# Output projections and late fillers of a two-block transformer kernel: from one fp32 product to three products of split operands, with GpSimd making the fillers' low parts

## The reference

```python
h = rms_norm(x); parts = split(h @ w_in)              # layer 0: a_u a_v a_g, b_q b_k b_v b_g, m_q m_g
x = x + concat([y_a, y_b, y_m], -1) @ w_out           # layer 0 (out0), w_out is 1280 x 1024
h = rms_norm(x); parts = split(h @ w_in)              # layer 1: c_a c_b c_g, d_q d_kv d_g, m_q m_g
x = x + concat([y_c, y_d, y_m], -1) @ w_out           # layer 1 (out1)
x = x + mix(retention(x), rg_lru(x)) @ w_out_2        # block 2
x = x + (gelu(conv(h @ up_g)) * (h @ up_v)) @ down    # feed-forward, then a last rms_norm
```

## Time and profile before

| | |
|---|---|
| median of 3 runs | 931.94 us (930.04 to 932.48) |
| the profiled execution | 932.02 us, of which 930.2 us lie between its first and last instruction |
| TensorE busy with matmuls | 889.6 us, 96% of the span |
| VectorE, ScalarE, GpSimd busy | 587.6, 389.7, 103.2 us |
| granted TensorE clock, mean | 0.992 |

### The profile page before, as it was taken

How to read it: one execution, slowest core, us unless ns; L and a number is a source line. 1 busy time by engine, 2 the same in 40 slices (tenths; PEclk the granted TensorE clock), 3 DMA queues, 4 the chain that set the end, 5 groups by cost and what they waited for, 6 DMA issues and landing times.

```text
span 930.2 us, 15618 instructions
## 1 busy us (share of the span) xinstructions
PE 889.6 (96%) x6262; PEld 824.1 (89%) x6262; DVE 587.6 (63%) x1114; ACT 389.7 (42%) x703; POOL 103.2 (11%) x114
## 2 busy tenths in 40 slices
PE   6999999999999999999999999999999999999996
PEld 6998988788888777878899999999998999999994
DVE  4784686432788788721597458955665676676673
ACT  6456654012002155612445676445354344543451
POOL 0149660101011000200400000100000000000000
PEclk9999999999999899999999999999999999999999
DMA  9444323243433611140655243555453456645641
GB/s 368 162 176 137 94 89 113 114 159 116 176 138 137 268 50 46 47 151 1 227 172 191 91 136 137 181 185 177 159 188 115 147 169 220 206 157 183 223 140 46
DMA packets 37784, 139.38 MB, mean 150 GB/s; under 512 B 4304, under 2 KB 4432, under 8 KB 37456
## 3 DMA queue, kind: packets, MB, share of 16 engines
q1 hardware_dynamic: 37424, 136.90, 42.5%
q10 hardware_dynamic: 288, 1.48, 0.5%
HBM read 137.32 MB, written 1.05 MB: 149 GB/s over the span
## 4 chain that ended last, share of the span: by engine, by line
PE 79%; issue 8%; DVE 8%; ACT 3%; POOL 1%; DMA 1%; DVEq 0%; SPq 0%; ACTq 0%; POOLq 0%
PE psum L534 18%; PE psum L535 18%; PE psum L536 18%; PE psum L537 18%; PE psum L609 1%; PE psum L667 1%; PE psum L685 1%; ACT logits L1195 1%; PE psum L810 1%; DVE neg_max L1803 1%; DVE psum L1797 1%; PE psum L678 1%; POOL w_lo L2253 1%; DVE rows L1834 1%; DMA rows<-in_mem 1%
## 5 line engine op out<-in xcount | busy, mean ns | idle before, releaser
L1546 DVE TENSOR_TENSOR w_lo<-raw,w_hi 128x1024 fp32r<-128x1024 f32 x162 | 190.9, 1222 | 76.4 <-ACT w_hi L1107 75.5
L534 PE MATMUL psum<-first 128*128 128x256 f32 (+1 forms) x960 | 218.6, 385 | 4.9 <-ACT first L1145 2.2
L534 PEld LDWEIGHTS psum<-first 128*128 128x128 f32 x960 | 180.5, 194 | 31.2 <-ACT first L1145 2.8
L1107 ACT ACTIVATE w_hi<-raw 128x1024 fp32r<-128x1024 f32 x184 | 185.8, 1053 | 34.5 <-PE psum L537 26.2
L535 PE MATMUL psum<-h_hi,w_hi 128*128 128x256 f32 x704 | 199.5, 283 | 0.6 <-issue 0.6
L537 PE MATMUL psum<-h_hi,w_lo 128*128 128x256 f32 x704 | 199.2, 283 | 0.0
L536 PE MATMUL psum<-h_lo,w_hi 128*128 128x256 f32 x704 | 199.2, 283 | 0.0
L535 PEld LDWEIGHTS psum<-h_hi,w_hi 128*128 128x128 f32 x704 | 135.1, 192 | 1.6 <-issue 1.4
L536 PEld LDWEIGHTS psum<-h_lo,w_hi 128*128 128x128 f32 x704 | 135.1, 192 | 0.2
L537 PEld LDWEIGHTS psum<-h_hi,w_lo 128*128 128x128 f32 x704 | 135.1, 192 | 0.0
L535 PE MATMUL psum<-w_hi,h_hi 128*128 128x256 f32 x448 | 129.5, 289 | 0.0
(11 more groups left out here) (268 smaller groups left out, 1071.5 us busy)
## 6 DMA issues: line engine op xcount, KB each, us to landing
raw<-in_blocks SPq DMA_DIRECT2D x184, 512.0 KB, 4.2
first<-in_blocks SPq DMA_DIRECT2D x64, 512.0 KB, 4.5
w_late<-in_blocks SPq DMA_DIRECT2D x4, 512.0 KB, 5.7
early<-in_early SPq DMA_DIRECT2D x1, 1579.0 KB, 16.4
attention<-in_late ACTq DMA_DIRECT2D x1, 1376.0 KB, 6.7
rows<-in_mem SPq DMA_DIRECT2D x2, 512.0 KB, 4.3
x<-in_x SPq DMA_DIRECT2D x1, 1024.0 KB, 8.4
out_x<-h_rows SPq DMA_DIRECT2D x2, 512.0 KB, 2.6
```

Source lines behind the costliest of these rows:

```text
L534: return nc.tensor.matmul(out, lhs[0], rhs[0], start=start, stop=stop, skip_group_check=shared_bank)
L1107: nc.scalar.activation(split_part(w_hi, q), raw[:, q % RAW_SLOTS, :], ACT.Copy).then_inc(w_hi_ready, 1)
L1546: V.tensor_tensor(split_part(w_lo, q), raw[:, q % RAW_SLOTS, :], split_part(w_hi, q).bitcast(F32), ALU.subtract).then_inc(w_lo_vector, 1)
```

## The change

The ten halves of `out0` and `out1` and the four of `c_g` and `d_g` move from `WHOLE` to `HALVES`: they become split products. Their left operands are split too. `ya`, `yb` and `ym` are copied to a high part by ScalarE (`source_hi`), all of them, and VectorE makes the low part behind it (`source_lo`, two instructions for a pair of tiles). For the fillers, layer 1's `h` stays whole for the other projections (now in the block of `mem_t`); ScalarE copies it to `h_hi`, and GpSimd makes `h_lo` in eight operations behind the power of the norm `dk`. `kv1` stays a whole product but is loaded through `raw` (`RAW_WHOLE`). GpSimd makes the low parts of `c_g`, `d_g`, `out0_r`, `out0` 0, `out1_r`, `out1` 0 and no longer of the first three halves of `x_lru`, which VectorE takes over with the other `out` halves; `out0` 1 stands inside the norm `y_b`. Layer 1's fillers begin two units later (`FILL_FROM`).

```diff
+FILL_FROM = [0, 2]
-LOW_BESIDE_NORM = {"q": both_of(["m_qg0"]), "k": both_of(["b_v"])}
+LOW_BESIDE_NORM = {"q": both_of(["m_qg0"]), "k": both_of(["b_v"]), "y_b": [("out0", 1)]}
...
-WHOLE = (both_of(["kv0"]) + out_halves(0)
-         + both_of(["kv1"]) + CONV_IN + both_of(["d_q", "dkv1", "m_qg1", "cmp_w1", "dkv2", "c_g", "d_g"]) + out_halves(1))
-HALVES = (L0_SPLIT + both_of(["x_lru0", "x_lru1", "r_q", "r_k", "y_lru0", "y_lru1", "r_v0", "r_v1", "g_ret0", "g_ret1"]
+WHOLE = both_of(["kv0"]) + CONV_IN + both_of(["d_q", "dkv1", "m_qg1", "cmp_w1", "dkv2"])
+RAW_WHOLE = both_of(["kv1"])
+HALVES = (L0_SPLIT + out_halves(0) + RAW_WHOLE + both_of(["c_g", "d_g"]) + out_halves(1) + both_of(["x_lru0", "x_lru1", "r_q", "r_k", "y_lru0", "y_lru1", "r_v0", "r_v1", "g_ret0", "g_ret1"]
...
-WHOLE_RING = [9, 4, 5, 6, 7]
+WHOLE_RING = [4, 5, 6, 7, 2, 3]
...
-VECTOR_FROM = len(L0_SPLIT) + SPLIT_SLOTS
-VECTOR_LO = both_of(["b_q", "b_k", "m_qg0", "b_v"]) + HALVES[VECTOR_FROM:]
+GPSIMD_LO = both_of(L0_FILL + ["c_g", "d_g"]) + [("out0_r", 0), ("out0", 0), ("out1_r", 0), ("out1", 0)]
+LO_BY_NAME = both_of(["b_q", "b_k", "m_qg0", "b_v"]) + [("out0", 1)]
...
-    return min(total, total * (i + 1) // FILL_UNITS[layer])
+    return min(total, total * max(0, i + 1 - FILL_FROM[layer]) // (FILL_UNITS[layer] - FILL_FROM[layer]))
```

TensorE, `out_rest` (`out_project` likewise goes from `y_whole` to `h_t`), and the new wait ahead of layer 1's attention:

```diff
-                                          pick(h_whole, slice(None), k, slice(t * P, (t + 1) * P)),
+                                          pick(ym_t, slice(None), k, slice(t * P, (t + 1) * P)),
...
+            pe.wait_ge(h1_lo, 1)
```

ScalarE at layer 0's end:

```diff
-            source("ym0", h_whole[0][:, 0:2, :], 0.5)
-            source("ya0_0", y_whole[0][:, 0:2, :], 0.25)
-            source("yb0_0", y_whole[0][:, 4:6, :], 0.5 * (1.0 - LAM_INIT))
+            split_to(OUT[0] + 3)
+            source_hi("ym0", ym_t[0], 0.5)
+            for j in range(2):
+                source_hi(f"ya0_{j}", h_t[0][:, 2 * j:2 * j + 2, :], 0.25)
+            split_to(OUT[0] + 4)
+            for j in range(2):
+                source_hi(f"yb0_{j}", h_t[0][:, 4 + 2 * j:6 + 2 * j, :], 0.5 * (1.0 - LAM_INIT))
+            split_to(OUT[0] + 5)
```

ScalarE in layer 1's projections:

```diff
+            for n in range(2):
+                k = slice(n * KT // 2, (n + 1) * KT // 2)
+                ins = nc.scalar.activation(h_t[0][:, k, :], h_whole[0][:, k, :], ACT.Copy)
+            src_hi.mark(ins, "h1", act)
...
+            split_to(FILL1 + 1)
             for j, name in enumerate("kv"):
                 arrive(xpose, f"hid_{name}")
...
+            split_to(FILL1 + 2)
             copy_chunk("dkv2", rows[:, :, 1024:1304], (HC, 24))
+            split_to(FILL1 + 3)
             nc.scalar.activation(gates[:, :, :], rows[:, :, 1280:1304], ACT.Tanh, scale=0.5).then_inc(gates_tanh, 1)
```

VectorE at layer 0's end (layer 1's likewise):

```diff
-            source("ya0_1", y_whole[0][:, 2:4, :], 0.25)
+            source_lo("ym0", ym_t, 0, 0.5)
+            for j in range(2):
+                source_lo(f"ya0_{j}", h_t, 2 * j, 0.25)
...
-            source("yb0_1", y_whole[0][:, 6:8, :], 0.5 * (1.0 - LAM_INIT))
+            split_to(OUT[0] + 4)
+            for j in range(2):
+                source_lo(f"yb0_{j}", h_t, 4 + 2 * j, 0.5 * (1.0 - LAM_INIT))
+            split_to(OUT[0] + 5)
             recurrence_rate()
```

GpSimd, behind each power:

```diff
+                if name == "dk":
+                    src_hi.wait(pool, "h1")
+                    for k in range(KT):
+                        ins = nc.gpsimd.tensor_tensor(h_t[1][:, k, :], h_whole[0][:, k, :], h_t[0][:, k, :].bitcast(F32),
+                                                      ALU.subtract)
+                    ins.then_inc(h1_lo, 1)
```

More of the change, by code:

```diff
@@ L102, with split_turn, split_before, hi_count @@
 MEM_BLOCK = 8
-WHOLE_RING = [9, 4, 5, 6, 7]
+WHOLE_RING = [4, 5, 6, 7, 2, 3]
 WHOLE_BLOCK = [9, 5] + [WHOLE_RING[j % len(WHOLE_RING)] for j in range(len(WHOLE) - 2)]
 WHOLE_TURN = [WHOLE_BLOCK[:j].count(b) for j, b in enumerate(WHOLE_BLOCK)]
-def split_slot(j):
-    return (j + 2) % SPLIT_SLOTS
+OUT = [HALVES.index(out_halves(layer)[0]) for layer in range(2)]
+X2 = HALVES.index(("x_lru0", 0))
+FILL1 = HALVES.index(("c_g", 0))
+SPLIT_HALVES = [h for h in HALVES if h not in RAW_WHOLE]
+def split_turn(j):
+    return SPLIT_HALVES.index(HALVES[j])
+def split_slot(j):
+    return (split_turn(j) + 2) % SPLIT_SLOTS
+def split_before(j):
+    n = split_turn(j) - SPLIT_SLOTS
+    return HALVES.index(SPLIT_HALVES[n]) if n >= 0 else None
+def hi_count(q):
+    return 2 * split_turn(q // 2) + q % 2 + 1
 def whole_ahead(j):
@@ L433, in low_parts, with raw_left @@
         def low_parts(q):
-            mine = HALVES[q // 2] in VECTOR_LO
-            ahead = sum((h in VECTOR_LO) == mine for h in HALVES[:q // 2])
-            return (w_lo_vector if mine else w_lo_ready), 2 * ahead + q % 2 + 1
+            pool = HALVES[q // 2] in GPSIMD_LO
+            ahead = sum((h in GPSIMD_LO) == pool for h in SPLIT_HALVES[:split_turn(q // 2)])
+            return (w_lo_ready if pool else w_lo_vector), 2 * ahead + q % 2 + 1
+        def raw_left(q):
+            return half_done[q // 2] if HALVES[q // 2] in RAW_WHOLE else low_parts(q)
         def wait_half(eng, half):
@@ L1047, in load_whole @@
                 if 2 <= block < MEM_BLOCK and 2 <= j and (ahead is None or ahead < 2):
-                    last = max(i for i in range(len(L0_SPLIT)) if split_slot(i) == (block - 2) // 2)
+                    last = max(i for i in range(FILL1) if HALVES[i] not in RAW_WHOLE and split_slot(i) == (block - 2) // 2)
                     sp.wait_ge(*half_done[last])
@@ L1481, in split_to @@
                 while split[0] < min(n, len(HALVES)):
-                    j = split[0]
+                    half = HALVES[split[0]]
                     split[0] += 1
-                    if j >= VECTOR_FROM:
-                        own_low_parts(HALVES[j])
+                    if half in SPLIT_HALVES and half not in GPSIMD_LO and half not in LO_BY_NAME:
+                        own_low_parts(half)
             def arrive(ring, name):
```

93 lines of the change are left out of this document (54 added, 39 removed).

## The result

The changed kernel takes **951.6 us** against 931.0 (ratio 1.020, interval 1.018 to 1.022): slower, as forecast, but by 19 to 20 us and not by 7, and outside the range. The 951.6 is the median of four executions, one of which took 3958 us at a mean granted clock of 0.21; the ratio leaves it out, and the other three took 947.6 to 952.7 us, 950.5 in the middle. So what follows explains the 15.3 us by which the two profiled spans differ. The mean granted clock was 0.969 to 0.973 in the three executions of the first series and is 0.975 in the profiled one; more time at the lower clock may be the missing 3 us, but no trace shows it.

The account below looks back on a forecast made before the run. TensorE, busy for 96% of the span, was taken as the bound, except ahead of layer 1's attention, where VectorE's program sets the time. The terms summed to +6.7 on 932.0 us, so 938.7, range 927 to 945.

Parts of the forecast that it names:

- Products, -16.1: TensorE: fourteen halves turned from whole to split products, 1.15 us less each, 16.1 us less work.
- Handovers, +3.7: Layers' ends: high and low parts replace single copies, lengthening three TensorE waits by about 1.2 us each, +3.7.
- Late weights, +1.4: Layer 0: `out0_2`'s low parts come 1.1 us late; two more ScalarE high parts in its attention cost 0.3.
- Start of the attention, +12: Ahead of layer 1's attention: four GpSimd bursts delay VectorE, 0.48 us per instruction hit, +12 us in all.
- the fourth burst: GpSimd's eight operations for `d_g` 0 ahead of layer 1's attention, perhaps half of them hitting VectorE, +2 us.
- The sign of 6 to 9 us idle ahead of the first scores: Check in the trace: TensorE would stand 6 to 9 us ahead of layer 1's first attention scores.
- Inside layer 1's attention, +3: First units without fillers, about 2 us; three pairs of ScalarE high parts, about 0.3 each; GpSimd bursts; +3 (1 to 6).
- Norm x2, -0.7: Layer 1's end: GpSimd's low parts no longer run beside VectorE's diagonal in the norm x2, -0.7 us.
- The clock, +3.4: TensorE's clock drops behind two of three lengthened handovers, 1.7 us each, +3.4 (0 to 6.8).
- the low parts did not slip in: Rival that GpSimd's low parts slip in beside VectorE, a hit costing a quarter: 927 us, chance 0.18.
- the whole-instruction price: Rival that a GpSimd instruction blocks VectorE for its whole length, 0.69 us a hit, start 18: 944.7 us, chance 0.12.

Follow-up runs that it names:

- h_lo_early: parts_behind_copy with `h_lo` made 60 us earlier, right after x1 is turned, so its GpSimd burst leaves the start of layer 1's attention; 935.4 us.
- late_behind: parts_behind_copy with the fillers' high parts made later on ScalarE, so GpSimd's bursts for `c_g` 0, `c_g` 1 and `d_g` 0 begin after `kc_t`; 943.7 us.
- one_pair_back: parts_behind_copy with one of its five pairs put back: `out1_r`'s high parts again ahead of the copy for unit 34 in layer 1's attention; 944.3 us.
- parts_behind_copy: Changed kernel with five pairs of ScalarE high parts in the two attentions moved behind one copy each of the transposed scores; 937.6 us.
- clock_kept: Changed kernel with plain matmuls, results unused, put on TensorE in six of its waits; 952.4 us.
- outs_only: Changed kernel with only output projections split: fillers whole, no `h_lo`, block order changed, high parts of `out1_r` and `out1` 0 later; 936.0 us.
- start_kept: parts_behind_copy with plain matmuls, written to a free bank, in four TensorE waits at the start of layer 1's attention; 942.4 us.
- vector_parts: parts_behind_copy with the low parts of `c_g` and `d_g` made by VectorE instead of GpSimd; 948.2 us.
- before_delayed: Kernel before the change, with two idle ScalarE copies ahead of one copy in each layer's attention (units 14 and 34), no product changed; 941.3 us.

## Why the prediction was off

- **Products, -16.1:** right. 144 records took 17.51 us at full clock (17.3 forecast).
- **Handovers, +3.7:** right. The waits are 1.99 us at both layers (2.1 forecast), and 1.70 instead of 0.79 ahead of `out1_r` (+0.9; 1.2 forecast).
- **Late weights, +1.4: the first step that failed,** in its second half. "Two more high parts fall on ScalarE in layer 0's attention ... +0.3" was an average over six pieces of before. What counts is between which instructions a piece stands: this one stood ahead of a copy that TensorE was about to need, behind a wait of 1.60 us that the trace of before showed. It cost 1.86 us, and 1.5 of clock. The average was also misapplied: 1.5 us over six pieces is 0.5 for two, not 0.3. `out0_2` cost 2.0 instead of 1.1.
- **Start of the attention, +12:** right in size and in what bounds it, 11.7. Inside it two errors met: the fourth burst cost 0.7 and not 2, and the slow clock lengthened VectorE's chain by 0.8, for which there was no term. The sign of 6 to 9 us idle ahead of the first scores did not hold (2.31). h_lo_early shows the price of one burst alone (3.4 us), late_behind that of the other three together with the clock (9.0).
- **Inside layer 1's attention, +3: the second and larger failure.** "About 0.3 each" for three pairs of high parts. They cost 0.48 us, 1.48 us and nothing as waits; what the term left out is that the clock comes down around such a wait. The second of them, with the low stretch around it, made 5.5 us (one_pair_back against parts_behind_copy), and with the clock held up the attention was 5.4 us shorter (clock_kept). With all five pairs behind their copies D to E is 83.3 us, where my terms give 82.2.
- **Norm x2, -0.7:** E to F is within 0.4 of the forecast; the diagonal takes 0.48 us, as in the earlier trace rows without GpSimd.
- **The clock, +3.4:** one drop behind a handover does cost about what I took (E to F is 38.2 us in outs_only, where it falls there, and 36.7 in the change; 1.5 against 1.7). But I put the drops in the wrong places, and took each to be 1.7 us wherever it falls. In the profile of the change none fell at a lengthened handover, and one stretch inside layer 1's attention lasted 17 us.

The two failures are one, a piece of work priced by an average and not by its place: 3.1 + 7.6 us. Changing the order takes 3.4 and 6.4 of them back, and the kernel then measures 937.6 us, where my sum was 938.7. The nearness is partly luck: the late weights and the attention come out about 1 us dearer each than summed, and the clock's 3.4 were not lost where I put them. Of the rivals, the low parts did not slip in, and hits of about 0.5 us fit better than the whole-instruction price: a rope instruction went from 0.22 to 0.76 us, and with 18 us the start would have been 115 us long, not 109.

Left open: why the clock fell late at layer 0's end in some executions and not in others with the same program there, and why the low stretch around the wait of 2.08 us lasts 3.4 us in some traces and 13.6 to 17 in others.

## What to carry to other kernels

Before you add work to an engine that is "40% busy", look between which two of its instructions it will stand, and who waits for the second one; here moving five such pieces behind one copy each was worth 10 us. A wait can cost more than its length, because the clock can come down with it and stay down; how long, one trace does not tell, so compare several. And matmuls put into a wait to hold the clock gained 1.5 and 5.4 us in the attentions, but lost where another engine ended last, and where they themselves had to wait.

## What the hardware showed that I had not expected

- TensorE's clock: the same wait of 2.08 us came with 3.4 us at 1.2 GHz in parts_behind_copy, h_lo_early and start_kept; with 17 us in the change and in one_pair_back, where a wait of 1.48 us stood behind it with 0.9 us of work between them; and with 13.6 us in late_behind and vector_parts, where no second wait did. So a second wait close behind is not needed for a long stretch, and layer 0's pair (1.60 and 1.86 us) brought only 3.4 us. In before_delayed the clock fell behind a wait of 1.29 us, and with one of 1.73 us coming 6 us later it was low for 17 us too. These are one trace for each kernel.
- A VectorE instruction with one input is hit by GpSimd too: `COPY logits<-kvc` 15x128 took 0.65 to 0.70 us in start_kept, and 0.21 beside no burst. The Trainium skill (SBUF — State Buffer, Who interferes with whom) says that a copy can contend when it runs in a mode with two ports; these rows agree that a copy is held up, and do not show its mode.
- A hit costs a short instruction as much as a long one, about 0.5 us: 0.22 became 0.76 in the rope, and 0.16 became 0.69 for 15 partitions of 16 elements.
